# Two decoder blocks on one core: activation transposes moved into the next weight unit, TensorE's code after the experts written in both branches, and the compressed keys computed with split weights from the weight ring

## The reference

```python
def swiglu(h, w_in, w_out):                      # FFN1 and FFN2, inner width 2816
    gate, up = jnp.split(h @ w_in, 2, axis=-1)
    return (jax.nn.silu(gate) * up) @ w_out

def compress_kv(kv, pos, w1, b1, w2, b2):        # keys and values, 15 overlapping spans of 32 tokens
    chunks = kv.reshape(2, B, n_chunk, CMP_STRIDE, G, Dh)
    w1r = w1.reshape(2, r, CMP_STRIDE, Dh, CMP_HIDDEN)
    pre = b1[:, None, None, None, :]
    for j in range(r):
        pe = pos[:, None, None, j * CMP_STRIDE:(j + 1) * CMP_STRIDE, None, :]
        part = jnp.einsum('kbnpgd,kpdh->kbngh', chunks + pe, w1r[:, j])
        pre = pre + part[:, :, j:j + n_cmp]
    hid = jax.nn.silu(pre)
    return jnp.einsum('kbcgh,khd->kbcgd', hid, w2) + b2[:, None, None, None, :]

def hybrid_layer(x, ...):
    x = x + 0.5 * swiglu(rms_norm(x, ffn1_norm), ffn1_w_in, ffn1_w_out)
    proj = rms_norm(x, mix_norm) @ w_mix_in      # queries, keys, values, gates
    ...                                          # three attentions, one over the compressed keys
    x = x + mix @ w_mix_out
    x = x + 0.5 * swiglu(rms_norm(x, ffn2_norm), ffn2_w_in, ffn2_w_out)
```

## Time and profile before

| | us |
|---|---|
| median of three runs | 1060.5 |
| the profiled execution | 1060.7 |
| its span | 1058.7 |
| PE busy in it | 1012.6 |
| DVE, ACT busy | 734.1, 609.1 |
| FFN1 (first matmul to first mixer matmul) | 528.03 to 719.24 |
| mixer units to first attention matmul | 719.24 to 782.89 |

### The profile page before, as it was taken

How to read it: one execution, slowest core, us unless ns; L and a number is a source line. 1 busy time by engine, 2 the same in 40 slices (tenths; PEclk the granted TensorE clock), 3 DMA queues, 4 the chain that set the end, 5 groups by cost and what they waited for, 6 DMA issues and landing times.

```text
span 1058.7 us, 13638 instructions
## 1 busy us (share of the span) xinstructions
PE 1012.6 (96%) x5237; PEld 844.4 (80%) x5237; DVE 734.1 (69%) x813; ACT 609.1 (58%) x694; POOL 51.7 (5%) x47
## 2 busy tenths in 40 slices
PE   7999999997899999999799999999998898999998
PEld 6788788787788888877578888897877687888887
DVE  5534885678999999999955556566487755555664
ACT  6476433538899999988743443345375345344331
POOL 0011561011000000000000000000000000000000
PEclk9999999997999999999999999999899999999999
DMA  8923444452999999999946555873420044555511
GB/s 297 336 83 120 134 145 150 148 186 85 320 373 386 387 386 386 386 386 387 346 145 202 195 191 167 281 271 126 157 80 2 1 159 164 197 194 193 174 70 40
DMA packets 117021, 223.29 MB, mean 211 GB/s; under 512 B 6426, under 2 KB 12713, under 8 KB 116970
## 3 DMA queue, kind: packets, MB, share of 16 engines
q1 hardware_dynamic: 116426, 221.08, 60.2%
q0 software_dynamic: 384, 1.24, 0.3%
q10 hardware_dynamic: 160, 0.27, 0.1%
HBM read 221.49 MB, written 1.07 MB: 210 GB/s over the span
## 4 chain that ended last, share of the span: by engine, by line
PE 79%; DVE 8%; DMA 7%; ACT 4%; issue 2%; DVEq 0%; ACTq 0%; SPq 0%
PE ps L1830 18%; PE ps L1832 18%; PE ps L1831 18%; DMA w_raw<-in_w_exp_gate 6%; PE ps L2127 5%; PE ps L2128 5%; DVE w_lo L965 3%; ACT w_hi L537 2%; PE ps L2151 2%; PE ps L2168 1%; PE ps L2381 1%; PE ps L1996 1%; DMA w_raw<-in_w_exp_down 1%; PE ps L1876 1%; PE ps L1825 1%
## 5 line engine op out<-in xcount | busy, mean ns | idle before, releaser
L965 DVE TENSOR_TENSOR w_lo<-w_raw,w_hi 128x2048 fp32r<-128x2048 f32 x204 | 464.7, 2289 | 144.3 <-ACT w_hi L537 140.6
L537 ACT ACTIVATE w_hi<-w_raw 128x2048 fp32r<-128x2048 f32 x204 | 390.9, 1917 | 215.8 <-PE ps L1832 199.5
L1830 PE MATMUL ps<-w_hi,h_hi 128*128 128x512 f32 (+1 forms) x704 | 273.6, 389 | 9.7 <-DVE h_lo L992 6.7
L1831 PE MATMUL ps<-w_lo,h_hi 128*128 128x512 f32 (+1 forms) x704 | 268.8, 382 | 0.0
L1832 PE MATMUL ps<-w_hi,h_lo 128*128 128x512 f32 (+1 forms) x704 | 268.7, 382 | 0.0
L1830 PEld LDWEIGHTS ps<-w_hi,h_hi 128*128 128x128 f32 x704 | 133.3, 189 | 38.0 <-issue 11.7
L1832 PEld LDWEIGHTS ps<-w_hi,h_lo 128*128 128x128 f32 x704 | 133.2, 189 | 26.0
L1831 PEld LDWEIGHTS ps<-w_lo,h_hi 128*128 128x128 f32 x704 | 133.4, 189 | 23.8
L1830 PE MATMUL ps<-w_hi,aT_hi 128*128 128x512 f32 x176 | 68.9, 391 | 0.0
L1832 PE MATMUL ps<-w_hi,aT_lo 128*128 128x512 f32 x176 | 68.5, 389 | 0.0
L1831 PE MATMUL ps<-w_lo,aT_hi 128*128 128x512 f32 x176 | 68.5, 389 | 0.0
(11 more groups left out here) (354 smaller groups left out, 1276.3 us busy)
## 6 DMA issues: line engine op xcount, KB each, us to landing
w_raw<-in_ffn_w_in SPq DMA_DIRECT2D x44, 1024.0 KB, 5.1
w_raw<-in_w_exp_gate SPq DMA_DIRECT2D x32, 1024.0 KB, 10.7
w_raw<-in_w_exp_up SPq DMA_DIRECT2D x32, 1024.0 KB, 9.8
w_raw<-in_w_exp_down SPq DMA_DIRECT2D x32, 1024.0 KB, 10.8
w_raw<-in_w_in SPq DMA_DIRECT2D x22, 1024.0 KB, 7.8
w_raw<-in_ffn_w_out SPq DMA_DIRECT2D x22, 1024.0 KB, 5.0
w_raw<-in_w_mix_in SPq DMA_DIRECT2D x8, 1024.0 KB, 6.3
w_raw<-in_w_out SPq DMA_DIRECT2D x4, 1024.0 KB, 5.0
```

The costliest lines, as they stand in the source:

```text
L537: act.activation(w_hi[:, u % SPLIT, :], w_raw[:, u % RAW, :], ACT.Copy).then_inc(hi_ready, 1)
L965: dve.tensor_tensor(w_lo[:, u % SPLIT, :], w_raw[:, u % RAW, :], w_hi[:, u % SPLIT, :], ALU.subtract).then_inc(lo_ready, 1)
L1830: pe.matmul(out, hi, w_h, start=first, stop=False)
L1831: pe.matmul(out, hi, w_l, start=False, stop=False)
```

## The change

1. **Transposes by one unit later.** `transpose_a` leaves the end of chunk 0 and of each turn of the loop, and stands inside the first unit of the next turn, behind 18 of its 24 matmuls (inside `narrow` after the loop, behind 24 of 48). ACT's and DVE's parts follow: `aT_hi_out` and `aT_lo_out` now stand first in the loop. DVE's `gated` of chunk 0 now stands behind `split_lo(u0 + 5)`.
2. **Experts' end.** Only the left half of `x` is transposed before FFN1; the right half is transposed inside FFN1's first unit. And PE's whole code from FFN1 on is a function, `behind_experts`, that stands once in the `If` and once in the `Else`.
3. **Compressed keys.** `cmp_w1` comes as two units of the ring (`U_CMP`), each by two loads of 0.5 MB, and is split like other weights; the mixer has ten units. ACT writes the keys' high part into `kv_cmp` (4 operations on 64x480), DVE the low part (4 more, and 4 small ones for the positions, where it had 5 copies before). `kv_cmp` is the stationary side, and each unit makes 16 matmuls of 256 columns, one unit before and one after unit (2, 1). DVE copies the sums out, and two small matmuls inside unit (3, 0) fold high and low parts (`fold_sums`). ACT's silu (`hidT`) moves behind `leave_mix(2)`.

```diff
@@ SP: the loads @@
-            sp.dma_start(cmp_w1, a["cmp_w1_2"][0].rearrange("k (pp q) h -> q k pp h", q=P)).then_inc(cmp_in, 16)
+            def cmp_load(half):
+                u = U_CMP[half]
+                sp.wait_ge(lo_ready, u - RAW + 1)
+                dst = w_raw[:, u % RAW, :].rearrange("p (pp k h) -> p pp k h", k=2, h=P)
+                for kv, landed in enumerate((raw_in[u % RAW], cmp_in)):
+                    sp.dma_start(dst[:, :, kv], a["cmp_w1_2"][0, kv].rearrange("(pp q) h -> q pp h", q=P)[:, 8 * half:8 * half + 8]
+                                 ).then_inc(landed, 16)
@@ ACT: chunks @@
                 split_hi(u0 + 5)
-                aT_hi_out(c0)
                 split_hi(u0 + 6)
                 s0 = u0 + 4
                 with act.Fori(0, n - 1) as i:
+                    aT_hi_out(i + c0)
                     split_hi(s0 + 3, i)
...
-                    aT_hi_out(i + (c0 + 1))
                     split_hi(s0 + 8, i)
+                aT_hi_out(c0 + n - 1)
@@ ACT: mixer @@
             split_hi(U_MIX + 4)
-            split_hi(U_MIX + 5)
+            act.wait_ge(cmp_in, 48)
+            split_hi(U_CMP[0])
+            act.wait_ge(kv_T, 1)
+            for g in range(2):
+                for odd in range(2):
+                    act.activation(kv_of(0, g, odd), kv_src(g, odd), ACT.Copy).then_inc(kv_hi, 1)
             leave_mix(1)
@@ DVE: chunks @@
                 split_lo(u0 + 4)
+                split_lo(u0 + 5)
                 gated(c0, u0 + 3)
-                split_lo(u0 + 5)
-                aT_lo_out(c0)
                 split_lo(u0 + 6)
@@ DVE: mixer @@
-                dve.tensor_copy(kvT[0:DH, :, g, :], src).then_inc(kvT_ready, 1)
-                dve.tensor_copy(kvT[DH:P, :, g, 0:S - 1], src[:, :, 1:S]).then_inc(kvT_ready, 1)
+                dve.wait_ge(kv_hi, 2 * g + 2)
+                for odd in range(2):
+                    dve.tensor_tensor(kv_of(1, g, odd), kv_src(g, odd), kv_of(0, g, odd), ALU.subtract).then_inc(kvT_ready, 1)
@@ PE: chunks, experts' end, compression @@
-                transpose_a(c0)
                 s0 = u0 + 4
                 with pe.Fori(0, n - 1) as i:
-                    unit(s0, (0, 1), 0, True, False, i)
+                    unit(s0, (0, 1), 0, True, False, i, inside=lambda: transpose_a(i + c0))
...
-                    transpose_a(c)
-            adds = ffn(U_FFN1, N_EXP, adds + 8, 13)
+                sums = ffn(U_FFN1, N_EXP, adds + 8, 13, lambda: turn_sums(1))
...
             with pe.If(is_few > 0):
                 few_experts()
-                turn_sums()
+                turn_sums(0)
+                behind_experts()
             with pe.Else():
...
-                    i = pe.matmul(ps[:, 4, 64 * kv:64 * kv + 3 * N_CMP], cmp_w1[:, kv, pp, :],
-                                  kvT[:, kv, :, 2 * pp:2 * pp + CMP_STRIDE * (N_CMP - 1) + 1:CMP_STRIDE],
-                                  start=(pp == 0), stop=(pp == PAIRS - 1))
+                def compress(half):
+                    pe.wait_ge(lo_ready, U_CMP[half] + 1)
+                    for n in range(PAIRS // 2):
+                        pp, wc = 8 * half + n, slice(2 * P * n, 2 * P * (n + 1))
+                        rows = kv_cmp[:, pp].rearrange("p l k c -> p (l k c)")
+                        pe.matmul(ps[:, 4, 0:2 * P], rows, w_hi[:, U_CMP[half] % SPLIT, wc], start=(pp == 0), stop=False)
+                        i = pe.matmul(ps[:, 4, 0:2 * P], rows, w_lo[:, U_CMP[half] % SPLIT, wc], start=False, stop=(pp == PAIRS - 1))
+                    i.then_inc(unit_used, 1)
```

More of the change, by code:

```diff
@@ L2248, in _ @@
                 last_down(u, N_EXP - 1, adds)
[L2249 to L2282, removed]
-                            i = product(ps[:, 4 + 2 * half + tt, :], h_hi[:, 6 + k, t], h_lo[:, 6 + k, t], w_hi[:, (u + 4) % SPLIT, wc],
-                                        w_lo[:, (u + 4) % SPLIT, wc], k == 0, k == 1)
-                        if half != tt:
-                            i.then_inc(down_half, 1)
-                i.then_inc(unit_used, 1)
-                return adds + 8
@@ L2326, in _ @@
-            i.then_inc(kv_T, 1)
-            pe.wait_ge(wr_split_lo, 2)
-            for k in range(KT):
-                i = product(ps[0:GATE_COLS, 5, 0:S], wr_hi[:, k, :], wr_lo[:, k, :], h_hi[:, k, :], h_lo[:, k, :], k == 0, k == KT - 1)
-            i.then_inc(gates_T, 1)
-            pe.wait_ge(mix_out, 2)
-            mix_unit(2, 0)
-            pe.wait_ge(gateT_set, 1)
-            for tt in range(TT):
-                i = pe.transpose(ps[:, 5, S + 32 * tt:S + 32 * tt + GATE_COLS], gate_T[:, tt * P:(tt + 1) * P], ident[0:GATE_COLS, 0:GATE_COLS])
@@ L2336, in _ @@
-            i.then_inc(gates_T, 1)
-            pe.wait_ge(cmp_in, 32)
-            pe.wait_ge(kvT_ready, 5)
-            for kv in range(2):
-                for pp in range(PAIRS):
-                    i = pe.matmul(ps[:, 4, 64 * kv:64 * kv + 3 * N_CMP], cmp_w1[:, kv, pp, :],
-                                  kvT[:, kv, :, 2 * pp:2 * pp + CMP_STRIDE * (N_CMP - 1) + 1:CMP_STRIDE],
-                                  start=(pp == 0), stop=(pp == PAIRS - 1))
-            i.then_inc(pre_T, 1)
-            mix_unit(2, 1)
@@ L2346, in _ @@
-            pe.wait_ge(mix_out, 4)
-            mix_unit(3, 0)
-            pe.wait_ge(hid_ready, 1)
-            for kv in range(2):
-                for g in range(2):
-                    o = ps[0:N_CMP, 4, kv * P + g * DH:kv * P + (g + 1) * DH]
-                    pe.matmul(o, hidT[:, kv, g * N_CMP:(g + 1) * N_CMP], cmp_w2[:, kv, :], start=True, stop=False)
-                    i = pe.matmul(o, one_row[:, 0:N_CMP], b2_row[:, kv, :], start=False, stop=True)
-            i.then_inc(kvc_ready, 1)
@@ L2450, in keep_warm @@
-            def keep_warm(n):
-                for _ in range(n):
-                    pe.matmul(ps[:, 3, :], h_hi[:, 0, 0:P], h_hi[:, 0:2, :].rearrange("p a s -> p (a s)"), start=True, stop=True)
-            pe.wait_ge(q_set, 2)
-            pe.wait_ge(k_set, 1)
-            pe.wait_ge(kcT_set, 1)
-            pe.wait_ge(mix_out, 6)
-            for s in range(ITEMS + 3):
-                if s < ITEMS:
-                    between(s)
-                    logits_of(s)
-                if s == 2:
-                    keep_warm(9)
-                if 2 <= s < ITEMS + 2:
-                    transpose_p(s - 2)
-                if s >= 3:
-                    if s == 3:
-                        pe.wait_ge(q_set, 4)
-                    weighted(s - 3)
@@ L2486, in _ @@
-            unit(U_MIXOUT + 3, (2, 3), 4, False, True, inside=first_half)
-            def second_half():
-                pe.wait_ge(tok_ready, 14)
-                transpose_cols(x, ident, (2, 3), (4, 5, 6, 7))
-            ffn(U_FFN2, N_EXP + FFN_FULL + 1, adds + 4, 25, second_half)
+                turn_sums(0)
+                behind_experts()
         @block.gpsimd
```

434 lines of the change are left out of this document (275 added, 159 removed).

## The result

The changed kernel took **1052.2 us** (median of 4 executions, 1049.3 to 1053.7); the kernel before took 1060.7 on the same chip. The ratio is 0.990 (95% interval 0.985 to 0.994); it is taken over all executions and is not the quotient of the two medians. A second series of 11 executions on another chip gave 1053.4 against 1061.1, ratio 0.992 (0.989 to 0.994). The forecast was 1049.1, range 1045.8 to 1054: the sign was right, the gain is about 8 us and not 11.4 (8.5 between these medians, 7.7 between those of the second series and between the two spans). The median lies in the range, but above the 1047 to 1051.5 that the forecast gave as its own. The profiled execution took 1053.22 with a span of 1051.0 (before 1060.7 and 1058.7).

What follows compares the result with a forecast made beforehand. PE was taken to bound the kernel, time being gained where it idles, repeats work or runs at half clock. Terms -5.3 - 1.75 - 4.65 + 0.3 = -11.4 against 1060.7 gave 1049.1 us, range 1045.8 to 1054.

Steps and rivals of the forecast that it cites:

- PE waits for its own code: Experts' end: the branch over the `Else` holds FFN1's first matmul; without it the start is 523.5 instead of 528.03, -4.5.
- The pause is then 2.1 us instead of 5.2, so I take full clock: FFN1's start: the shorter pause leaves no matmuls at half clock, another -1.7 us.
- E: Stretch from FFN1's first transposes to the mixer's first matmul; forecast -5.3, bounds -6.75 without wait, -3 with half clock.
- The right half inside costs 0.80 and a wait of 1.45 before unit 4: FFN1's chunk 0: the right half's 8 transposes take 0.80 us of PE, and PE waits some 1.45 before unit 4.
- FFN2 -1.75: FFN2's chunk 0: the 2.56 us of wait for `gated` and transposes go, 0.80 stays, so -1.75.
- R: Stretch from the first logits read to the start of the last addition; forecast -1.75.
- Mixer -4.65: Mixer to attention: ACT and DVE carry the chain, first logits read at 780.4 instead of 785.06, -4.65.
- End +0.3: Program's end: PE's branch over the `Else` now follows the last matmul; cost between 0 and 2 us, taken as 0.3.
- The fetch stays: Rival, experts' end: straight code comes through the same full DMA engines, PE stands until 528; 1053.8 us, chance 0.10.
- slower by fetches at the loops' branches: Rival, FFN loops: each branch back needs a fetch of 2.6 us, 15.6 in all; 1064.7 us, chance 0.03.
- ACT and DVE hold the mixer, perhaps with half clock at the experts' end: Rival, mixer: their strided operations take twice the time, -2 to -4 less gain; about 1052 us, chance 0.17.
- Z: Stretch from the start of the last addition to the end of the span; forecast +0.3.

Runs made afterwards that it cites:

- run 2: Kernel before, with only PE's code behind the experts copied into both branches, both halves of x transposed ahead as before: 1058.2 us, ratio 0.997.
- 4: Changed kernel with PE's code behind the experts once, behind both branches; right half of x still inside the first unit: 1057.6 us, ratio 0.993.
- run 9: Changed kernel without PE's other branch (code for many chosen experts, not run with these inputs): 1050.5 us, ratio 0.990.
- 7: Changed kernel with ACT making unit 4's high half before FFN1's first silu, not behind it: 1053.2 us, ratio 0.991.
- run 5: Changed kernel with both halves of x transposed before FFN1's first unit: 1051.1 us, ratio 0.989.
- 1: Kernel before, with only the chunks' transposes moved inside the next chunk's first unit and the first narrow unit: 1060.2 us, ratio 0.998.
- 3: Changed kernel with chunks, joined code and both halves as before, leaving only the compressed keys' part: 1058.5 us, ratio 0.996.
- 6: Changed kernel with 7 unused matmuls of 512 columns in PE's pause before FFN1's first unit: 1053.3 us, ratio 0.991.
- 8: Changed kernel whose other branch, not run with these inputs, leaves out the second copy of PE's code: 1052.5 us, ratio 0.990.
- 11: Changed kernel with both halves ahead, DVE's gain on the first keys before a split, and unused matmuls in attention items 9 to 12: 1052.3 us, ratio 0.991.

## Why the prediction was right, and where it was not

- *PE waits for its own code; without the branch it begins 0.2 us behind the first step of `h_lo`.* Right: that the branch holds the start is shown (2, 4). That the time goes into fetching code is what the packet of the instruction queue suggests; it takes 1.1 of the 5.2 us (3.5% of 16 engines in 2 us), and no run shows what the rest is. Forecast 523.5, measured 523.75 on a time line that stood 0.24 later.
- *"The pause is then 2.1 us instead of 5.2, so I take full clock."* This step failed: 1.65 us. A pause of 2.06 us brought a fall in 3 of 5 profiled executions. A shorter pause was taken for a harmless one, though the same edit took 8 transposes out of it, which in run 2 cut it to 0.66 us. E was forecast at -5.3 and came to -3.41, near its bound of -3 for half clock; in run 9, where the clock stayed, it is -5.06.
- *The right half inside costs 0.80 and a wait of 1.45 before unit 4.* Right in mechanism and nearly in size (1.28), by the very chain named: right half, squares, reciprocals, silu, split (7). What the forecast didn't see is that this price bought nothing: with both halves ahead the start is the same (2, 5).
- *FFN2 -1.75.* Right: R is -1.75, and FFN1 gives 1.53 (1).
- *Mixer -4.65.* Right: -4.53. From ACT leaving unit (2, 1) to the root for the heads it took 9.1 us (756.41 to 765.53; counted 9.5), from there to the first logits 11.8 (counted 11.7). PE's wait before attention was 1.3, counted 2, and for the split in unit (2, 1) 0.25, counted 0, a small case of what the prediction had named as a sign of being wrong. The clock didn't fall.
- *End +0.3.* Mis-sized: +1.75, near the upper bound. The rows could have given it: from PE's last instruction to the next a jump takes 5.2 us. PE's last matmul now ends at 1045.96, and the span 5.04 later. What was hidden of it are the 3.3 us in which the last addition and the stores run anyway. The prediction gives no reason for taking 0.3 out of its 0 to 2.
- *Rivals.* "The fetch stays" and "slower by fetches at the loops' branches" didn't come: no loop has a gap at its branch. "ACT and DVE hold the mixer, perhaps with half clock at the experts' end", some 1052, had the right time for half of its reasons: the half clock came, the longer mixer didn't. It was a rival with a chance of 0.17, so the time alone would have spoken for it and not for the forecast.

The miss in numbers: -11.4 + 1.9 (E) + 0.1 (M) + 1.45 (Z) = -7.9, which is the table's sum.

Open: why the clock falls in attention in some profiled executions (3, 4, 6, 7, 8, 11) and not in others. With R from 268.6 to 273.7 this is large enough to hide what run 5 gains; that it makes the whole spread of the times is not shown. A variant of the changed kernel that is shorter than it by more than the measurement's uncertainty was not found; run 5 is the best candidate by its stretches.

## What to carry to other kernels

Price a far jump as a time from the engine's last instruction to its next (5.0 to 5.3 us here), and subtract what has to be waited for anyway: at the experts' end 4.5 us of it showed, at the program's end 1.75. When a pause shrinks, ask what stood in it: here 8 transposes inside the pause cost nothing and the clock stayed up, and moved behind it they brought their own time, a wait and in 3 of 5 executions a fall of the clock. Add up stretches of the trace; where single edits are worth 0.2%, the medians can't tell them apart.

## What the runs showed of the hardware

- The jump took 5.19 (before) and 5.29 us (4) of idle at the experts' end, and 5.04 from the last matmul to the end of the span in the changed kernel, where the packet itself took about 0.9 us. In all three the DMA engines were full for the first 1.5 to 3 us and less busy behind, so whether their load sets the price is open.
- The Trainium skill (Runtime: NRT & Kernel Launch, section on instruction fetch mechanics) has the rule that a taken branch to code outside what is fetched forces a fetch by DMA. The trace agrees: each of these jumps has a packet of the instruction queue behind it, and run 9, without a jump, has none at its end.
- The granted clock fell to 0.50 (1.2 GHz) while TensorE was busy without a gap in the old compression, in 3 of 3 profiled kernels that had it (run 2's row below); in 11 of 11 with the same product as 256-column matmuls it stayed at 1.00.

```profile
753.00:757.00 4.00, 4.00 (x14) 3.42 (x14) 0.16 (x1) 0.46 (x2) 0.00 (x0) 0.50 0.30 111
```

- ACT's and DVE's operations that write 64x480 elements in the strided order of the compression took 1.04 and 1.09 us each, where a copy of 64x512 into rows took 0.69 (before, below). The operations differ in kind as well (a copy on ScalarE, a subtraction of two inputs on VectorE), so how much of it the stride costs is not shown.

```profile
744.48 0.69 DVE L1585 COPY arena<-ps 64x512 f32<-64x512 f32 x1
```
